# The last layer norm of a decoder step: sample tile in fifth place, small operations once per group, bias and gain spread over POOL and VectorE

## The chip, the cores and the metric

The kernel runs on one core of a Trainium2 chip. The metric is the device time of one execution in microseconds (us), as the median of several runs of the whole program. The five engines of the core run side by side and meet only at semaphores: TensorE (PE), VectorE (DVE), ScalarE (ACT), GpSimd (POOL) and SyncE (SP), which here issues the DMA transfers between HBM and the on-chip memory.

## The reference, cut to what matters

One layer of a decoder: a mixer, a layer norm, a mixture of experts and a second layer norm, for a prompt of 2048 rows and for 8 x 8 = 64 sample rows, each row 1024 wide. The change touches the last line only:

```python
u2 = x * (1.0 + sc2[:, None]) + sh2[:, None]
y_moe = _hier_moe(u2, w_group, b_group, w_route, b_route, w_gate, w_up, w_down)
x = _layer_norm(ALPHA * x + (1.0 + g2[:, None]) * y_moe, ln2_g, ln2_b)
# _layer_norm: (x - mean) * rsqrt(var + LN_EPS) * g + b, over each row
```

## The kernel before

The program is written engine by engine: every engine has its own instruction list (the functions under `@block.sync`, `@block.gpsimd`, `@block.scalar`, `@block.vector`, `@block.tensor`), and its order is the order of the code. Semaphores join them. `o.step` issues an instruction and makes its engine wait until it has finished; `o.did` only counts it, and `o.wait` waits later.

The stages follow one another: modulation vectors, projections and recurrence in eight chunks, output projection with the first layer norm, routing, 48 slots of 128 rows through the experts, and the last stage, which is the one changed. In the slots POOL scatters each result row into the residual sum `z_d` in HBM (prompt rows are added there) or into `ysamp_d` (the two expert results of each sample row). The last stage waits until all of it has landed.

The last stage works on NT = 17 tiles of up to 128 rows x 1024, each in its own buffer `zt[t]`. Tiles 0 to 15 are the prompt, tile 16 has the 64 sample rows. For one tile:

1. SP loads it (line 487; sample rows line 488, and their two expert results `y_pair` line 490). All loads are issued at the start, in the order of the tiles, the sample rows last; SP waits for the last scatter into `ysamp_d` (`yr0`, `yr1`) ahead of load 13.
2. DVE takes its statistics (`f_stats`): two `bn_stats` of 512 columns (line 1434), `bn_aggr` (1437) and adding epsilon to the variance (1438). For the sample tile three operations on 64 x 1024 stand ahead: the sum of the two expert results (1430), times the gate `g2_s` (1431), plus the residual rows (1432).
3. ACT takes the root (`root`, 918). DVE forms the reciprocal and minus mean times reciprocal (`f_scale`, 1444 and 1445).
4. ACT normalizes the tile (`norm_z`, 922), POOL multiplies it by the row `ln2_g` (`scale_o`, 662), DVE adds the row `ln2_b` (`f_out`, 1451), and SP stores it (494; the sample tile 496).

On DVE the steps of three tiles are interleaved by hand: statistics of tile t, scale of tile t-1, bias of tile t-2.

```python
            for t in range(2, NT):
                f_stats(t, P if t < NT - 1 else NS)
                f_scale(t - 1)
                f_out(t - 2)
            f_scale(NT - 1, NS)
            f_out(NT - 2)
            f_out(NT - 1, NS)
```

POOL and ACT go through the tiles in order; a semaphore that counts up (`frs_ready`, `fnorm`, `fg_ok`, `fo_ok`) tells each how far the one before it is. SP's stores wait in the same order.

Of the kernel before, what the change touches and what calls it, by code (L numbers as in the profile page):

```python
# [5 lines left out]
P = 128  # L6
D = 1024
KD = D // P
SEQ, DEC_B, DEC_T = 2048, 8, 8
NS = DEC_B * DEC_T  # L10
NTOK = SEQ + NS
# [25 lines left out]
LN_EPS = 1e-5  # L37
LRU_C = 8.0
# [46 lines left out]
def build(nc, A):  # L85
    with ExitStack() as ctx:
# [37 lines left out]
        def part_at(off, *shape):  # L124
# [138 lines left out]
            fg_ok fo_ok fo_stored""".split()}  # L263
# [37 lines left out]
        def _(sp):  # L301
# [200 lines left out]
        def _(pool):  # L502
# [156 lines left out]
            def scale_o(t, n=P):  # L659

                pool.wait_ge(S["fnorm"], t + 1)
# [3 lines left out]
            for t in range(NT):  # L665
                scale_o(t, P if t < NT - 1 else NS)
# [3 lines left out]
        def _(act):  # L670
# [245 lines left out]
            def root(t, n=P):  # L916
                act.wait_ge(S["fvar_ready"], t + 1)
                act.activation(sd_z[0:n, t:t + 1], mv_z[0:n, t, 1:2], ACT.Sqrt).then_inc(S["fsd_ready"], 1)

            def norm_z(t, n=P):  # L920
                act.wait_ge(S["frs_ready"], t + 1)
                act.activation(zt[t][0:n, :], zt[t][0:n, :], ACT.Identity, bias=rs_z[0:n, t, 1:2],  # L922
                               scale=rs_z[0:n, t, 0:1]).then_inc(S["fnorm"], 1)

            root(0)
            for t in range(1, NT):
                root(t, P if t < NT - 1 else NS)
                norm_z(t - 1)
            norm_z(NT - 1, NS)


        @block.vector
        def _(dve):
# [490 lines left out]
            def f_stats(t, n=P):  # L1424

                dve.wait_ge(z_in[t], 16)
# [6 lines left out]
                for h in range(2):  # L1433
                    o.did(dve.bn_stats(st6[t % 2][0:n, h, :], zt[t][0:n, 512 * h:512 * h + 512]))  # L1434
# [364 lines left out]
```

## Time and profile before

| | |
|---|---|
| median of 3 runs | 1424.78 us (1421.13 to 1426.93) |
| the profiled execution | 1424.33 us |
| its span in the profile | 1422.6 us |
| last stage in the profile, from the first statistics to the end of the last bias | 1346.50 to 1419.22 us |
| busy in the whole span | PE 1184.7, DVE 901.3, ACT 535.7, POOL 545.4 us |
| busy from 1342.0 us to the end (80.6 us) | PE 0.0, DVE 68.1, ACT 24.5, POOL 40.6 us |

Times in a view are us from the start of the span, durations are us, mean durations of a group are ns. A row of a timeline gives the start, the duration, the engine, the line of the kernel, the operation, what it writes and reads, and in brackets how long the engine had stood idle and what ended that. The last stage is about 5% of the span, and no matrix product runs in it.

### The profile page before, as it was taken

To read this page: it belongs to the slowest core of one execution; us is meant where nothing else is said; L and a number is where in the kernel's file an instruction comes from. 1 tells how busy PE (TensorE), PEld (TensorE's weight loads), DVE (VectorE), ACT (ScalarE), POOL (GpSimd) and SP (SyncE) were. 2 spreads that over 40 slices of the span, in tenths; PEclk is the share of its full clock that TensorE was granted. 3 is DMA by queue.
4 is the path that set the end of the run, shared out by engine and by line. 5 is a ranking of instruction groups with operands and counts; after the bars stand their busy time and mean duration, and the time that the engine had idled before them with its cause. 6 is when DMAs were issued, how large, how long until landed. Compare 5 with 4: busy or idle time off the path is not lost. (4 is left out here: it accounts for less than half of the span.)

```text
span 1422.6 us, 23126 instructions
## 1 busy us (share of the span) xinstructions
PE 1184.7 (83%) x6473; PEld 952.0 (67%) x6474; DVE 901.3 (63%) x1824; ACT 535.7 (38%) x915; POOL 545.4 (38%) x545
## 2 busy tenths in 40 slices
PE   6697899999999866799999418999999999999400
PEld 1122699999999765688887317778778787788300
DVE  1114659898899848555655595556676666643398
ACT  0200453535544360222222204445556545533232
POOL 1012022112222043556565243455565455444264
PEclk9897899999999888899999658999999999999755
DMA  8990011011111055244444408888899798654582
GB/s 260 363 349 4 1 38 59 16 43 59 59 59 43 16 183 180 94 147 162 144 162 134 154 15 290 217 216 207 231 268 269 203 269 207 147 111 97 133 310 111
DMA packets 114671, 214.47 MB, mean 151 GB/s; under 512 B 17669, under 2 KB 67337, under 8 KB 114597
## 3 DMA queue, kind: packets, MB, share of 16 engines
q1 hardware_dynamic: 93903, 163.20, 33.5%
q0 software_dynamic: 20736, 50.89, 16.2%
q8 instruction: 15, 0.25, 0.1%
q14 instruction: 17, 0.14, 0.0%
HBM read 153.36 MB, written 85.96 MB: 168 GB/s over the span
## 5 line engine op out<-in xcount | busy, mean ns | idle before, releaser
L1523 PE MATMUL bank<-parts 128*128 128x256 f32 (+2 forms) x1616 | 570.0, 353 | 37.4 <-POOL parts L567 17.5
L1525 PE MATMUL bank<-parts 128*128 128x256 f32 (+2 forms) x1616 | 553.0, 342 | 0.0
L1524 PE MATMUL bank<-parts 128*128 128x256 f32 (+2 forms) x1616 | 552.3, 342 | 0.0
L1523 PEld LDWEIGHTS bank<-parts 128*128 128x128 f32 x1616 | 309.0, 191 | 78.5 <-issue 20.8
L1525 PEld LDWEIGHTS bank<-parts 128*128 128x128 f32 x1616 | 308.4, 191 | 35.6
L1524 PEld LDWEIGHTS bank<-parts 128*128 128x128 f32 x1616 | 309.3, 191 | 31.9
L1470 PE MATMUL bank<-ident,arena 128*128 128x128 f32 (+4 forms) x788 | 118.3, 282 | 26.2 <-DVE arena L1166 8.5
L1470 PEld LDWEIGHTS bank<-ident,arena 128*128 128x128 f32 (+4 forms) x788 | 94.3, 147 | 54.9 <-issue 11.6
L545 POOL TENSOR_TENSOR arena<-arena 128x256 f32<-128x256 f32 (+1 forms) x36 | 26.1, 728 | 270.3 <-DVE h_last L1082 247.5
L1351 DVE TENSOR_TENSOR parts<-arena,parts x90 | 104.8, 1220 | 17.9 <-ACT parts L855 17.9
L880 ACT ACTIVATE arena<-bank,w_now 128x512 f32<-128x512 f32 x96 | 66.1, 689 | 127.3 <-PE bank L1525 73.0
L1497 PE MATMUL bank<-ada_arena,cT 128*9 128x512 f32 x192 | 87.0, 615 | 18.3 <-DMA ada_arena<-in_w_ada 18.3
L1385 DVE SCALAR_TENSOR_TENSOR arena<-bank,w_now,arena 128x512 f32<-128x512 f32 x96 | 69.2, 749 | 49.8 <-PE bank L1525 49.8
L855 ACT ACTIVATE parts<-arena x90 | 88.7, 1056 | 4.9 <-DMA arena<-in_w_down 4.9
L633 POOL DMA_INDIRECT z_d<-arena,dst_now x48 | 80.8, 1684 | 19.3 <-issue 19.3
L703 ACT ACTIVATE arena<-bank,proj_b 128x256 f32<-128x256 f32 x64 | 30.4, 475 | 142.4 <-PE bank L1525 142.4
L585 POOL TENSOR_TENSOR arena<-arena 128x1024 f32<-128x1024 f32 (+1 forms) x17 | 57.0, 3350 | 52.2 <-ACT arena L804 52.2
L1139 DVE TENSOR_TENSOR arena<-bank,arena 128x512 f32<-128x512 f32 (+1 forms) x34 | 21.8, 683 | 86.2 <-PE bank L1525 86.2
L1497 PEld LDWEIGHTS bank<-ada_arena,cT 128*9 128x9 f32 x192 | 17.6, 93 | 85.9 <-issue 85.9
L1358 DVE TENSOR_TENSOR parts<-bank,parts 128x512 fp32r<-128x512 f32 x96 | 61.8, 685 | 7.8 <-ACT parts L860 7.8
L860 ACT ACTIVATE parts<-bank 128x512 fp32r<-128x512 f32 x96 | 52.2, 596 | 35.9 <-PE bank L1470 33.5
L567 POOL TENSOR_TENSOR parts<-arena,parts 128x1024 fp32r<-128x1024 f32 (+1 forms) x17 | 44.9, 2643 | 49.8 <-ACT parts L791 49.8
(258 smaller groups left out, 1544.5 us busy)
## 6 DMA issues: line engine op xcount, KB each, us to landing
ada_arena<-in_w_ada SPq DMA_DIRECT2D x12, 2048.0 KB, 11.0
arena<-in_w_gate SPq DMA_DIRECT2D x16, 1024.0 KB, 5.8
arena<-in_w_up SPq DMA_DIRECT2D x16, 1024.0 KB, 9.4
arena<-in_w_down SPq DMA_DIRECT2D x16, 1024.0 KB, 13.1
arena<-in_x_prompt SPq DMA_DIRECT2D x8, 1024.0 KB, 6.6
yT_d<-arena SPq DMA_DIRECT2D x16, 512.0 KB, 4.4
arena<-yT_d SPq DMA_DIRECT2D x16, 512.0 KB, 4.7
arena<-in_x_prompt SPq DMA_DIRECT2D x16, 512.0 KB, 3.3
```

The source lines that it names most:

```text
L585: o.step(pool.tensor_tensor(x1[b][0:n, :], z[b][0:n, :], row_tiles[0:n, 1, :], ALU.mult))
L633: pool.indirect_dma_start(out=z_d, out_offset=bass.IndirectOffsetOnAxis(ap=dst_now[b][:, 0:1], axis=0), in_=y_sb[b], in_offset=None, compu ...
L855: act.activation(part(w_hi, e & 1, n), raw_part(e & 1, n), ACT.Copy).then_inc(S["w_hi"], 1)
L880: act.activation(y_raw[b][:, 512 * h:512 * h + 512], bank[5 + h][:, :], ACT.Copy, scale=w_now[b][:, 0:1]).then_inc(S["y_act"], 1)
L1351: dve.tensor_tensor(part(w_lo, e & 1, n), raw_part(e & 1, n), part(w_hi, e & 1, n).bitcast(F32), ALU.subtract).then_inc(S["w_lo"], 1)
L1358: dve.tensor_tensor(xT_lo[:, k, :], bank[h][:, :].rearrange("p (k n) -> p k n", n=P), xT_hi[:, k, :].bitcast(F32), ALU.subtract).then_inc( ...
L1385: dve.scalar_tensor_tensor(y_sb[b][:, cols], bank[5 + h][:, :], w_now[b][:, 0:1], g2_row[:, cols], ALU.mult, ALU.mult).then_inc(S["y_dve"], 1)
L1470: return pe.transpose(out, in_, ident[0:rows, 0:rows])
L1497: last = pe.matmul(bank[n][0:NM, :], cT[:, k, :], w_ada[n][:, k, :], start=k == 0, stop=k == KD - 1)
L1523: pe.matmul(out, x_hi, w_hi, start=start, stop=False)
L1524: pe.matmul(out, x_hi, w_lo, start=False, stop=False)
L1525: return pe.matmul(out, x_lo, w_hi, start=False, stop=stop)
```

## The change

All in the last stage. A position q from 0 to 16 takes the place of the tile number in the semaphores and in the small arrays; `FIN_TILES` says which tile stands there.

- **Order.** The sample tile is worked fifth (q = 4). Its loads are issued fifth too, and with them goes the wait for the scatters into `ysamp_d`.
- **Groups.** Adding epsilon, root, reciprocal and minus mean times reciprocal run once for a group of 4, 4, 4, 3 and 2 tiles instead of once per tile, on as many columns. `mv_z` is set to 1.0 beforehand, because the grouped operations read all 128 rows of the sample's column.
- **Lag.** DVE's bias of a tile stands five tiles behind its statistics.
- **Bias on POOL.** For q = 2, 5, 8, 11 POOL also adds the bias, right behind its multiply.
- **Last tile on DVE.** For q = 16 DVE multiplies by `ln2_g` and adds the bias; POOL leaves this tile out.

```diff
+FIN_TILES = (0, 1, 2, 3, 16, *range(4, 16))
+FIN_GROUPS = ((0, 4), (4, 8), (8, 12), (12, 15), (15, 17))
+FIN_LAG = 5
+FIN_DVE_GAIN = (16,)
+FIN_POOL_BIAS = (2, 5, 8, 11)
...
-            for t in range(NT - 1):
-                if t == 13:
+            for q, t in enumerate(FIN_TILES):
+                if t < NT - 1:
+                    sp.dma_start(zt[t], x1_t[t]).then_inc(z_in[q], 16)
+                else:
                     for b in range(2):
                         sp.wait_ge(S[f"yr{b}"], 16 * (SLOTS // 2))
-                sp.dma_start(zt[t], x1_t[t]).then_inc(z_in[t], 16)
-            sp.dma_start(zt[NT - 1][0:NS, :], z_d[SEQ:NTOK, :]).then_inc(z_in[NT - 1], 16)
-            for k in range(2):
-                sp.dma_start(y_pair[k][0:NS, :], ysamp_d[k * NS:(k + 1) * NS, :]).then_inc(pair_in, 16)
-            for t in range(NT):
-                sp.wait_ge(S["fo_ok"], t + 1)
+                    for k in range(2):
+                        sp.dma_start(y_pair[k][0:NS, :], ysamp_d[k * NS:(k + 1) * NS, :]).then_inc(pair_in, 16)
+                    sp.dma_start(zt[t][0:NS, :], z_d[SEQ:NTOK, :]).then_inc(z_in[q], 16)
+            for q, t in enumerate(FIN_TILES):
+                if q in FIN_POOL_BIAS:
+                    sp.wait_ge(S["fo_pool"], FIN_POOL_BIAS.index(q) + 1)
+                else:
+                    sp.wait_ge(S["fo_ok"], q + 1 - sum(n < q for n in FIN_POOL_BIAS))
...
+            def affine_o(q, t, n=P):
+
+                pool.wait_ge(S["fnorm"], q + 1)
                 pool.tensor_tensor(zt[t][0:n, :], zt[t][0:n, :], ln2_g[0:n, :], ALU.mult).then_inc(S["fg_ok"], 1)
+                if q in FIN_POOL_BIAS:
+                    pool.wait_ge(S["fg_ok"], q + 1)
+                    pool.tensor_tensor(zt[t][0:n, :], zt[t][0:n, :], ln2_b[0:n, :], ALU.add).then_inc(S["fo_pool"], 1)
...
+            def roots_z(i, lo, hi):
+                act.wait_ge(S["fvar_ready"], i + 1)
+                act.activation(sd_z[:, lo:hi], mv_z[:, lo:hi, 1], ACT.Sqrt).then_inc(S["fsd_ready"], 1)
+
+            def norms_z(i, lo, hi):
+                act.wait_ge(S["frs_ready"], i + 1)
+                for q in range(lo, hi):
...
+                o.did(dve.bn_aggr(mv_z[0:n, q, :], st6[q % 2][0:n, :, :].rearrange("p a b -> p (a b)")))
+
+            def f_vars(lo, hi):
+
+                o.wait()
+                dve.tensor_scalar(mv_z[:, lo:hi, 1], mv_z[:, lo:hi, 1], LN_EPS / (ALPHA * ALPHA), None,
                                   ALU.add).then_inc(S["fvar_ready"], 1)
 
+            def f_scales(i, lo, hi):
+
+                dve.wait_ge(S["fsd_ready"], i + 1)
+                o.step(dve.reciprocal(rs_z[:, lo:hi, 0], sd_z[:, lo:hi]))
+                dve.scalar_tensor_tensor(rs_z[:, lo:hi, 1], mv_z[:, lo:hi, 0], -1.0, rs_z[:, lo:hi, 0],
                                          ALU.mult, ALU.mult).then_inc(S["frs_ready"], 1)
 
+            def f_out(q, t, n=P):
+
+                if q in FIN_DVE_GAIN:
+                    dve.wait_ge(S["fnorm"], q + 1)
+                    dve.tensor_tensor(zt[t][0:n, :], zt[t][0:n, :], ln2_g[0:n, :], ALU.mult).then_inc(S["fg_dve"], 1)
+                    dve.wait_ge(S["fg_dve"], FIN_DVE_GAIN.index(q) + 1)
+                else:
+                    dve.wait_ge(S["fg_ok"], q + 1)
+                if q not in FIN_POOL_BIAS:
+                    dve.tensor_tensor(zt[t][0:n, :], zt[t][0:n, :], ln2_b[0:n, :], ALU.add).then_inc(S["fo_ok"], 1)
+
+            o.step(dve.memset(mv_z[:], 1.0))
             dve.wait_ge(S["fin_in"], 32)
-            f_stats(0)
-            f_stats(1)
-            f_scale(0)
-            for t in range(2, NT):
-                f_stats(t, P if t < NT - 1 else NS)
-                f_scale(t - 1)
-                f_out(t - 2)
-            f_scale(NT - 1, NS)
-            f_out(NT - 2)
-            f_out(NT - 1, NS)
+            out = 0
+            for i, (lo, hi) in enumerate(FIN_GROUPS):
+                for q in range(lo, hi):
+                    f_stats(q, FIN_TILES[q], P if FIN_TILES[q] < NT - 1 else NS)
+                    if q == hi - 1:
+                        f_vars(lo, hi)
+                    while out <= q - FIN_LAG:
+                        f_out(out, FIN_TILES[out], P if FIN_TILES[out] < NT - 1 else NS)
+                        out += 1
+                f_scales(i, lo, hi)
+            while out < NT:
+                f_out(out, FIN_TILES[out], P if FIN_TILES[out] < NT - 1 else NS)
+                out += 1
```

The order of the instructions shows at three places what moved. The names in square brackets are the semaphores an instruction waits for; `st`, `mv_z`, `sd_z` and `rs_z` hold the statistics, `arena` the tiles, `ada_arena` the two expert results of the sample rows.

On DVE, one round of the loop before, here for the tile in place 2:

```order
L1434 BN_STATS st_0<-arena 128x6 [waits z_in2]
L1434 BN_STATS st_0<-arena 128x6
L1436 MEMSET spare 1x1 [waits dve_order]
L1437 BN_AGGR mv_z<-st_0 128x2
L1438 TENSOR_SCALAR mv_z<-mv_z 128x1 [waits dve_order]
L1444 RECIPROCAL rs_z<-sd_z 128x1 [waits fsd_ready]
L1445 SCALAR_TENSOR_TENSOR rs_z<-mv_z,rs_z 128x1 [waits dve_order]
L1451 TENSOR_TENSOR arena<-arena 128x1024 [waits fg_ok]
```

On DVE in the change, from the end of the first group to the first bias:

```order
L1451 BN_AGGR mv_z<-st_1 128x2
L1456 TENSOR_SCALAR mv_z<-mv_z 128x4 [waits dve_order]
L1462 RECIPROCAL rs_z<-sd_z 128x4 [waits fsd_ready]
L1463 SCALAR_TENSOR_TENSOR rs_z<-mv_z,rs_z 128x4 [waits dve_order]
L1444 TENSOR_TENSOR ada_arena<-ada_arena 64x1024 [waits pair_in,fin_s_in,z_in4]
L1445 TENSOR_TENSOR ada_arena<-ada_arena,arena 64x1024 [waits dve_order]
L1446 TENSOR_TENSOR arena<-arena,ada_arena 64x1024 [waits dve_order]
L1448 BN_STATS st_0<-arena 64x6 [waits dve_order]
```

The scale of the first tile stands behind the statistics of four tiles instead of two, and the three sample operations follow it at once, with the biases behind them.

On DVE, the end of the program before:

```order
L1451 TENSOR_TENSOR arena<-arena 128x1024 [waits fg_ok]
L1430 TENSOR_TENSOR ada_arena<-ada_arena 64x1024 [waits pair_in,fin_s_in,z_in16]
L1431 TENSOR_TENSOR ada_arena<-ada_arena,arena 64x1024 [waits dve_order]
L1432 TENSOR_TENSOR arena<-arena,ada_arena 64x1024 [waits dve_order]
L1434 BN_STATS st_0<-arena 64x6 [waits dve_order]
```

And in the change:

```order
L1451 BN_AGGR mv_z<-st_0 128x2
L1456 TENSOR_SCALAR mv_z<-mv_z 128x2 [waits dve_order]
L1462 RECIPROCAL rs_z<-sd_z 128x2 [waits fsd_ready,fg_ok]
L1463 SCALAR_TENSOR_TENSOR rs_z<-mv_z,rs_z 128x2 [waits dve_order]
L1475 TENSOR_TENSOR arena<-arena 128x1024 [waits fg_ok] x4
L1470 TENSOR_TENSOR arena<-arena 128x1024 [waits fnorm]
L1475 TENSOR_TENSOR arena<-arena 128x1024 [waits fg_dve]
```

Four biases, a multiply and a fifth bias now end the program on DVE; the sample operations are gone from there.

On POOL, the last stage before, with the last scatters ahead of it:

```order
L633 DMA z_d<-arena,dst_now 2240x1024
L635 DMA ysamp_d<-arena,dst_now 128x1024
L662 TENSOR_TENSOR arena<-arena 128x1024 [waits fnorm,fin_in]
L662 TENSOR_TENSOR arena<-arena 128x1024 [waits fnorm] x15
L662 TENSOR_TENSOR arena<-arena 64x1024 [waits fnorm]
```

And in the change:

```order
L671 TENSOR_TENSOR arena<-arena 128x1024 [waits fnorm,fin_in]
L671 TENSOR_TENSOR arena<-arena 128x1024 [waits fnorm] x2
L674 TENSOR_TENSOR arena<-arena 128x1024 [waits fg_ok]
L671 TENSOR_TENSOR arena<-arena 128x1024 [waits fnorm]
L671 TENSOR_TENSOR arena<-arena 64x1024 [waits fnorm]
L671 TENSOR_TENSOR arena<-arena 128x1024 [waits fnorm]
L674 TENSOR_TENSOR arena<-arena 128x1024 [waits fg_ok]
L671 TENSOR_TENSOR arena<-arena 128x1024 [waits fnorm] x3
L674 TENSOR_TENSOR arena<-arena 128x1024 [waits fg_ok]
L671 TENSOR_TENSOR arena<-arena 128x1024 [waits fnorm] x3
```

POOL has 20 operations of this size where it had 17: 16 multiplies and four biases.

## Rows read from the trace of the kernel before

**Rows 1.** The page: the chain that ended last, by engine.

```profile
DVE 5%; DMA 1%; PE 0%; issue 0%; POOL 0%; ACT 0%; DVEq 0%; POOLq 0%; SPq 0%
```

**Rows 2.** Timeline, one round of the last stage on DVE, ACT and POOL.

```profile
1357.61 1.22 DVE L1451 TENSOR_TENSOR arena<-arena 128x1024 f32<-128x1024 f32 x1
1357.63 1.24 ACT L922 ACTIVATE arena<-arena,rs_z 128x1024 f32<-128x1024 f32 x1 [0.64 <-DVE rs_z L1445]
1358.76 1.28 DVE L1434 BATCH_NORM_STATS2 st<-arena 128x6 f32<-128x512 f32 x2
1358.95 2.34 POOL L662 TENSOR_TENSOR arena<-arena 128x1024 f32<-128x1024 f32 x1 [1.37 <-ACT arena L922]
...
1360.31 0.15 DVE L1438 TENSOR_SCALAR mv_z<-mv_z 128x1 f32<-128x1 f32 x1
...
1360.57 0.73 DVE L1445 SCALAR_TENSOR_TENSOR rs_z<-mv_z,rs_z 128x1 f32<-128x1 f32 x1
1361.32 1.22 DVE L1451 TENSOR_TENSOR arena<-arena 128x1024 f32<-128x1024 f32 x1
```

**Rows 3.** Groups by line and shape, line 1445: count | busy us, mean ns | idle before.

```profile
L1445 DVE SCALAR_TENSOR_TENSOR rs_z<-mv_z,rs_z 128x1 f32<-128x1 f32 x16 | 11.9, 742 | 0.6
```

**Rows 4.** Timeline, the end of the last stage.

```profile
1403.29 1.21 DVE L1430 TENSOR_TENSOR ada_arena<-ada_arena 64x1024 f32<-64x1024 f32 x1
1403.48 3.22 POOL L662 TENSOR_TENSOR arena<-arena 128x1024 f32<-128x1024 f32 x1 [1.37 <-ACT arena L922]
1404.53 3.24 DVE L1431 TENSOR_TENSOR ada_arena<-ada_arena,arena 64x1024 f32<-64x1024 f32 x1
...
1412.38 4.63 POOL L662 TENSOR_TENSOR arena<-arena 128x1024 f32<-128x1024 f32 x2 [5.68 <-ACT arena L922]
1414.74 4.48 DVE L1451 TENSOR_TENSOR arena<-arena 128x1024 f32<-128x1024 f32 x2 [2.34 <-POOL arena L662]
1419.25 0.52 SPq L496 DMA_DIRECT2D result<-arena  x1
```

**Rows 5.** Lines 562 and 1076, earlier stage: durations ns min/median/max, first and last start.

```profile
L562 POOL TENSOR_TENSOR parts<-arena,parts x3: 2377/3342/3354, 524.8 to 530.4; 128x1024 fp32r<-128x1024 f32 x3
L1076 DVE TENSOR_TENSOR parts<-arena,parts x5: 1212/3370/3431, 525.6 to 535.9; 128x1024 fp32r<-128x1024 f32 x5
```

**Rows 6.** Timeline, the start of the last stage.

```profile
1346.50 1.29 DVE L1434 BATCH_NORM_STATS2 st<-arena 128x6 f32<-128x512 f32 x2 [10.56 <-DMA arena<-z_d]
1347.83 0.20 DVE L1437 BATCH_NORM_AGGREGATE mv_z<-st 128x2 f32<-128x12 f32 x1
...
1348.07 0.15 DVE L1438 TENSOR_SCALAR mv_z<-mv_z 128x1 f32<-128x1 f32 x1
1348.14 1.28 DVE L1434 BATCH_NORM_STATS2 st<-arena 128x6 f32<-128x512 f32 x2
...
1351.54 2.33 POOL L662 TENSOR_TENSOR arena<-arena 128x1024 f32<-128x1024 f32 x1 [11.78 <-ACT arena L922]
```

**Rows 7.** Timeline, first layer norm: from epsilon to the scale, DVE waiting for ACT.

```profile
763.04 0.15 DVE L1154 TENSOR_SCALAR mv<-mv 128x1 f32<-128x1 f32 x1
...
763.66 0.16 DVE L1157 SCALAR_TENSOR_TENSOR rs<-mv,rs 128x1 f32<-128x1 f32 x1
```

**Rows 8.** Half-microsecond stretches: busy us (count) by engine, PEclk, DMA share, GB/s.

```profile
1351.00:1351.50 0.50, 0.00 (x0) 0.00 (x0) 0.46 (x3) 0.39 (x1) 0.00 (x0) 0.50 0.99 410
...
1366.50:1367.00 0.50, 0.00 (x0) 0.00 (x0) 0.50 (x2) 0.00 (x0) 0.50 (x1) 0.50 1.03 213
```

**Rows 9.** Timeline of the DMA issues on SP, then issues by line, us to landing.

```profile
1342.85 8.77 SPq L487 DMA_DIRECT2D arena<-z_d  x16
...
result<-arena SPq DMA_DIRECT2D x1, 256.0 KB, 2.9
```

**Rows 10.** Timeline, routing stage: a tensor_scalar on 16 columns beside POOL's run.

```profile
816.32 14.42 POOL L606 TENSOR_TENSOR parts<-arena,parts 128x1024 fp32r<-128x1024 f32 x6 [18.76 <-ACT parts L842]
...
826.19 2.26 DVE L1253 TENSOR_SCALAR arena<-arena 128x16 f32<-128x16 f32 x1
```

More of the change, by code:

```diff
@@ L657, in _ @@
                 scatter(s, s % 2, (s + 1) // 2)
-            def scale_o(t, n=P):
-                pool.wait_ge(S["fnorm"], t + 1)
+            def affine_o(q, t, n=P):
+                pool.wait_ge(S["fnorm"], q + 1)
                 pool.tensor_tensor(zt[t][0:n, :], zt[t][0:n, :], ln2_g[0:n, :], ALU.mult).then_inc(S["fg_ok"], 1)
+                if q in FIN_POOL_BIAS:
+                    pool.wait_ge(S["fg_ok"], q + 1)
+                    pool.tensor_tensor(zt[t][0:n, :], zt[t][0:n, :], ln2_b[0:n, :], ALU.add).then_inc(S["fo_pool"], 1)
             pool.wait_ge(S["fin_in"], 32)
-            for t in range(NT):
-                scale_o(t, P if t < NT - 1 else NS)
+            for q, t in enumerate(FIN_TILES):
+                if q not in FIN_DVE_GAIN:
+                    affine_o(q, t, P if t < NT - 1 else NS)
         @block.scalar
@@ L913, in _ @@
             y_evac(s, 1, SLOTS // 2 - 1)
[L916 to L929, printed above, removed]
+            def roots_z(i, lo, hi):
[4 more added lines that the diff above has]
+                for q in range(lo, hi):
+                    t = FIN_TILES[q]
+                    n = P if t < NT - 1 else NS
+                    act.activation(zt[t][0:n, :], zt[t][0:n, :], ACT.Identity, bias=rs_z[0:n, q, 1:2],
+                                   scale=rs_z[0:n, q, 0:1]).then_inc(S["fnorm"], 1)
+            for i, (lo, hi) in enumerate(FIN_GROUPS):
+                roots_z(i, lo, hi)
+                norms_z(i, lo, hi)
         @block.vector
@@ L1433, in f_stats @@
                 for h in range(2):
-                    o.did(dve.bn_stats(st6[t % 2][0:n, h, :], zt[t][0:n, 512 * h:512 * h + 512]))
+                    o.did(dve.bn_stats(st6[q % 2][0:n, h, :], zt[t][0:n, 512 * h:512 * h + 512]))
                 o.wait()
                 dve.memset(spare[0:1, 0:1], 0.0)
-                o.step(dve.bn_aggr(mv_z[0:n, t, :], st6[t % 2][0:n, :, :].rearrange("p a b -> p (a b)")))
-                dve.tensor_scalar(mv_z[0:n, t, 1:2], mv_z[0:n, t, 1:2], LN_EPS / (ALPHA * ALPHA), None,
+                o.did(dve.bn_aggr(mv_z[0:n, q, :], st6[q % 2][0:n, :, :].rearrange("p a b -> p (a b)")))
@@ L1439, in f_stats @@
+            def f_vars(lo, hi):
+                o.wait()
+                dve.tensor_scalar(mv_z[:, lo:hi, 1], mv_z[:, lo:hi, 1], LN_EPS / (ALPHA * ALPHA), None,
                                   ALU.add).then_inc(S["fvar_ready"], 1)
-            def f_scale(t, n=P):
-                dve.wait_ge(S["fsd_ready"], t + 1)
-                o.step(dve.reciprocal(rs_z[0:n, t, 0:1], sd_z[0:n, t:t + 1]))
-                dve.scalar_tensor_tensor(rs_z[0:n, t, 1:2], mv_z[0:n, t, 0:1], -1.0, rs_z[0:n, t, 0:1],
+            def f_scales(i, lo, hi):
+                dve.wait_ge(S["fsd_ready"], i + 1)
+                o.step(dve.reciprocal(rs_z[:, lo:hi, 0], sd_z[:, lo:hi]))
+                dve.scalar_tensor_tensor(rs_z[:, lo:hi, 1], mv_z[:, lo:hi, 0], -1.0, rs_z[:, lo:hi, 0],
@@ new lines, in _ @@
+            o.step(dve.memset(mv_z[:], 1.0))
+            dve.wait_ge(S["fin_in"], 32)
+            out = 0
+            for i, (lo, hi) in enumerate(FIN_GROUPS):
+                for q in range(lo, hi):
[6 more added lines that the diff above has]
+                f_scales(i, lo, hi)
```

9 lines of the change are left out of this document (3 added, 6 removed).

## The prediction

> **What bounds the kernel now.** I read the chain that ended last first. Only its end matters for a change in the last stage, and there it runs on DVE alone: DVE holds 5% of the whole span, about the length of this stage, and POOL and ACT hold 0% [rows 1]. So by the chain the stage is bound by VectorE. The timeline of one round says what VectorE does in that time [rows 2]. The bias of a tile (1.22 us) starts at 1357.61 and the next at 1361.32, so a round takes 3.71 us. In it the scalar_tensor_tensor on one column (line 1445) shows 0.73 us. It should be small: it starts at 1360.57 and ends at 1361.30, and POOL's multiply, begun at 1358.95 and 2.34 us long, ends at 1361.29. All sixteen of these have a mean of 0.74 us [rows 3]. The operation stands still until POOL is done.
>
> The end of the stage shows the same with large operands [rows 4]. POOL asks for its multiply at 1403.48, while DVE adds two tiles until 1404.50; POOL takes 3.22 us instead of 2.34. DVE starts its next product at 1404.53 and takes 3.24 us: to POOL's end at 1406.70 and 1.07 us more. So **a DVE operation with two on-chip inputs and POOL's elementwise operation exclude each other**; each waits for the other's end. Statistics have one input and don't wait: they take their 1.28 us while a multiply runs [rows 2]. An earlier stage shows both engines with operations queued back to back: POOL's take up to 3.35 us, DVE's 3.37 in the median [rows 5]. That is one POOL operation and one DVE operation, about 2.27 and 1.10 us, in strict turn; neither is shut out.
>
> The resource that bounds the stage is therefore not VectorE but this turn-taking, which I call the port. A round of 3.71 us is 2.34 (POOL) + 1.22 (DVE) and 0.15 of gaps; the statistics and small operations lie beside POOL's multiply.
>
> **The change part by part.**
>
> *Small operations per group.* Twelve of the 17 sets of epsilon, root, reciprocal and line 1445 go. On DVE three of them cost about 0.15 us each, and line 1445 its wait. Beside POOL's multiply all of that is hidden, so their removal is worth only the gaps: in strict turn a round costs 3.37 us [rows 5] instead of 3.71, that is 0.34 us in each round where both engines have work queued. Whether they have is the question of the next steps.
>
> *Head.* Before, POOL starts at 1351.54 [rows 6]. Now four statistics come first. The first aggregate starts 1.33 us behind the statistics, which took 1.29 us there with POOL idle, and an instruction without a wait follows a small one by 0.07 us (1348.07 to 1348.14) [rows 6], so a tile takes about 1.41 us and the fourth aggregate starts at 1352.06; with a wait behind each (0.24 us) it would be 1352.5. Epsilon follows at 1352.3. From there to line 1445, with ACT's root between, the first layer norm took 0.62 us [rows 7]: 1352.9, done at 1353.05. ACT normalizes in 1.24 us [rows 2], and POOL asks at 1354.4, **2.9 us later** than before. For four columns instead of one I take the same durations.
>
> *Sample tile fifth.* Its three operations (3 x 1.22 us) leave the end, where POOL stood idle for 5.68 us [rows 4], and come to 1353. When has it landed? The first tile is there at 1346.50 [rows 6]. At 410 GB/s a 0.524 MB tile takes 1.28 us, the fourth is there at 1350.3. The sample transfers ran at 213 GB/s, last of all in the program before [rows 8]; 0.786 MB then take 3.6 us: 1353.9. SP issues 16 loads in 8.77 us [rows 9], fast enough. For the wait on `yr0` and `yr1`, moved from load 13 to load 4, the bounds are nothing and 5 us (load 13 was reached at about 1350, and no wait shows there); I take nothing, since it waits only for small scatters that were issued with those already waited for.
>
> So DVE begins the sample at 1353.9 and ends its first sum at 1355.15. POOL asked at 1354.4, as it did at 1403.48 [rows 4], and has the port next. The product and the last sum alternate with two multiplies (2 x 3.35 us): the sample rows are ready at 1361.85 where they would be at 1357.6 if nothing stood between.
>
> *From there to the second group.* Two statistics to 1364.7; bias 0 waits for POOL's first bias (q = 2), which runs from 1364.2 to 1366.5, and ends at 1367.6; statistics to 1369; bias 1 waits for multiply 3 and ends at 1371.0; statistics to 1372.4; small operations 0.24 + 0.62 + 0.16, ACT 1.24, gaps: POOL asks for multiply 4 at 1374.7. Its multiply 3 ended at 1369.9. **POOL is dry for 4.8 us**, the price of working in groups, of which bias 1 fills 1.1.
>
> *From 1374.7 to the end.* POOL has 12 multiplies (q = 4 to 15) and 3 biases, 15 x 2.3 = 34.5 us. DVE has ten biases, the last tile's multiply and its bias, 12 x 1.15 = 13.8. All 27 use the port: 48.3 us, or 1423.0. Before the third group POOL runs dry again: bias 6 waits for multiply 6, multiply 7 is already queued and goes first (as the second multiply did at about 1414.7, ahead of the bias waiting for the first [rows 4]), and the group's small operations come behind that bias. That leaves the port empty for about 1.7 us: 1424.7. At the last two groups a bias or queued multiplies bridge it.
>
> *Bias on POOL, last tile on DVE.* Both are in this sum. Four biases cost 2.3 us of the port on POOL instead of 1.15 on DVE: +4.6. The last tile's multiply goes the other way: -1.15.
>
> *Store.* The last store is a full tile instead of 64 rows; 2.9 us to landing before [rows 9]; I count no difference, with 1 us either way.
>
> *Sum.* The last bias ended at 1419.22 (1414.74 + 4.48 [rows 4]). The same accounting gives 1419.7 for the kernel before, so I take 0.5 off: 1424.2, **5.0 us later**. 1424.33 + 5.0 = 1429.3 for an execution like the profiled one, which lies 0.45 us below the median of the runs; I forecast **1429.0 us**, +0.3%. A measurement of this kernel tells apart about 0.5%, 7 us, so this counts as no change.
>
> **A rule that could move it.** Epsilon on one column took 0.15 us beside POOL's multiply [rows 2]: it didn't wait. On 16 columns the same operation took 2.26 us beside a run of POOL's [rows 10]: it did. The groups have 2 to 4 columns and lie between. I take the one-column row, the nearest. The Trainium skill, VectorE: DVE Perf Modes, section What auto-detection actually checks, says that a one-input operation uses both read ports if the outermost dimension that isn't one is even or equal in source and destination. By it the grouped epsilon would wait. In my schedule it meets a busy POOL at three of five groups, and the bias behind it waits for that same operation anyway; by the rule the sum would be under 1 us more.
>
> **The rivals.**
>
> *The port never stands empty.* If the sample lands by 1353.2, DVE's product comes ahead of POOL's first multiply, the sample is ready about 3 us sooner, and the second group is in time. At the limit all operations stand in one unbroken row from 1353.1: 20 x 2.3 + 17 x 1.15 = 65.6 us, end 1418.7, which is 0.5 us less than before, or 1424. For it speaks that only 0.7 us decides; against it the 213 GB/s. Between it and the forecast lie 1424 to 1426.5.
>
> *POOL runs dry at every group* (the slower side). The small operations of a group stand on DVE behind its last statistics, and in groups 3 and 4 behind a bias which waits for POOL. From aggregate to POOL's next operation it is 0.24 + 0.62 + 0.16 + 1.24 and gaps, 2.4 us. If the last three groups each pay it in full, where I charge 1.7 in all, that is 7.2 - 1.7 = +5.5: 1434.5. It decides where the group's epsilon starts less than 2.4 us before POOL's queue ends; the wait of [rows 10] at each group would push it there, and so would a late sample. Against it speak the biases on POOL at q = 8 and 11, which lengthen its queue just there.
>
> *The engines don't exclude each other with these operands.* Then POOL needs 1354.4 + 20 x 2.34 = 1401.2 and DVE about as long, with dry spells the end is near 1407, and the time 1412. The views in [rows 2 to 5] speak against it throughout.
>
> **How the numbers follow.** The forecast, 1426.5 to 1432, has 0.52; the port always full 0.27; dry at every group 0.17; no exclusion 0.04. Faster by over 0.5% (under 1417.7) comes from the last alone: 0.04. Slower by over 0.5% (over 1431.9) is the third: 0.17. Within: 0.79. The range goes from 1421.5, the full port less 2.5 us for the scatter of the runs, to 1434.5: outside lie the last rival and half of the third, and a little of the second.
>
> **What would show it.** The sample's product taking 3.2 us or more beside POOL's first multiply; POOL's first multiply at 1354 to 1355; a gap of 4 to 5 us on POOL ahead of its fifth multiply, a smaller one ahead of the ninth; biases on DVE of 1.2 to 3.4 us, never two POOL operations long; the last bias at about 1424. Wrong would be: POOL without gaps after its start (first rival), gaps at all four boundaries (second), or a POOL multiply of 2.34 us with a DVE addition wholly inside it (third).

## The result, and the profile after

| | before | changed |
|---|---|---|
| median of 18 runs each | 1423.08 us (1416.88 to 1426.93) | 1427.15 us (1423.82 to 1431.61) |
| the profiled execution, its span | 1424.33, 1422.6 us | 1426.49, 1424.6 us |
| last stage, first statistics to end of the last bias | 1346.50 to 1419.22, 72.72 us | 1343.93 to 1421.51, 77.58 us |

The ratio is 1.0033, with a 95% interval from 1.0021 to 1.0045: slower, by less than the 0.5% that the prediction counted as no change. The stage is 4.86 us longer. In this execution it begins 2.57 us earlier than in the one of before, so positions are compared below as distances from the stage's start.

In the chain that ended last, by engine, POOL has come in [rows 1]:

```profile
DVE 4%; DMA 1%; POOL 1%; PE 0%; ACT 0%; SPq 0%; issue 0%; DVEq 0%; POOLq 0%
```

The timeline of POOL in the last stage of the changed kernel (start, duration, line, operation, and in brackets the idle time before and what ended it; L671 is the multiply, L674 the bias; three of the four biases are left out):

```profile
1352.23 9.54 POOL L671 TENSOR_TENSOR arena<-arena 128x1024 f32<-128x1024 f32 x3 [15.10 <-ACT arena L938]
...
1364.14 3.33 POOL L671 TENSOR_TENSOR arena<-arena 128x1024 f32<-128x1024 f32 x1
1372.26 5.70 POOL L671 TENSOR_TENSOR arena<-arena 64x1024 f32<-64x1024 f32 x2 [4.79 <-ACT arena L938]
...
1381.21 4.64 POOL L671 TENSOR_TENSOR arena<-arena 128x1024 f32<-128x1024 f32 x2
1388.56 3.39 POOL L671 TENSOR_TENSOR arena<-arena 128x1024 f32<-128x1024 f32 x1 [2.72 <-ACT arena L938]
...
1394.34 7.91 POOL L671 TENSOR_TENSOR arena<-arena 128x1024 f32<-128x1024 f32 x3
1402.33 2.35 POOL L674 TENSOR_TENSOR arena<-arena 128x1024 f32<-128x1024 f32 x1
1404.64 12.26 POOL L671 TENSOR_TENSOR arena<-arena 128x1024 f32<-128x1024 f32 x4
```

Two brackets stand behind the start: POOL is dry for 4.79 us ahead of the second group's first multiply (the fifth) and for 2.72 ahead of the third group's (the ninth). At the last two groups there is none. Before, POOL had idled 1.37 us in each round [rows 2] and 5.68 at the sample tile [rows 4].

The timeline of DVE for the same stretch (L1444 to L1446 are the sample's three operations, L1456 the grouped epsilon, L1470 the gain of the last tile, L1475 the bias):

```profile
1343.93 1.29 DVE L1448 BATCH_NORM_STATS2 st<-arena 128x6 f32<-128x512 f32 x2 [10.58 <-DMA arena<-z_d]
...
1349.99 0.17 DVE L1456 TENSOR_SCALAR mv_z<-mv_z 128x4 f32<-128x4 f32 x1
...
1351.78 1.22 DVE L1444 TENSOR_TENSOR ada_arena<-ada_arena 64x1024 f32<-64x1024 f32 x1 [0.97 <-DMA arena<-z_d]
1353.03 3.26 DVE L1445 TENSOR_TENSOR ada_arena<-ada_arena,arena 64x1024 f32<-64x1024 f32 x1
1356.32 3.25 DVE L1446 TENSOR_TENSOR arena<-arena,ada_arena 64x1024 f32<-64x1024 f32 x1
...
1375.70 3.34 DVE L1475 TENSOR_TENSOR arena<-arena 64x1024 f32<-64x1024 f32 x1 [0.82 <-POOL arena L671]
...
1381.92 1.65 DVE L1456 TENSOR_SCALAR mv_z<-mv_z 128x4 f32<-128x4 f32 x1
1383.58 3.35 DVE L1475 TENSOR_TENSOR arena<-arena 128x1024 f32<-128x1024 f32 x1
...
1393.56 0.84 DVE L1456 TENSOR_SCALAR mv_z<-mv_z 128x3 f32<-128x3 f32 x1
...
1407.24 0.75 DVE L1456 TENSOR_SCALAR mv_z<-mv_z 128x2 f32<-128x2 f32 x1
...
1410.20 8.92 DVE L1475 TENSOR_TENSOR arena<-arena 128x1024 f32<-128x1024 f32 x4
1419.05 1.21 DVE L1470 TENSOR_TENSOR arena<-arena 128x1024 f32<-128x1024 f32 x1
1420.29 1.22 DVE L1475 TENSOR_TENSOR arena<-arena 128x1024 f32<-128x1024 f32 x1
```

The sample's product and last sum take 3.26 and 3.25 us, since POOL's first multiplies run beside them; alone on the port such an operation took 1.22 (line 1444). The gain and bias of the last tile, with POOL done, take 1.21 and 1.22. In the groups by line and shape of the same stage (count | busy us, mean ns | idle before) the waiting shows as length:

```profile
L671 POOL TENSOR_TENSOR arena<-arena 128x1024 f32<-128x1024 f32 (+1 forms) x16 | 46.8, 2945 | 22.6 <-ACT arena L938 22.6
...
L1475 DVE TENSOR_TENSOR arena<-arena 128x1024 f32<-128x1024 f32 x12 | 26.1, 2192 | 2.3 <-POOL arena L671 2.3
...
L1463 DVE SCALAR_TENSOR_TENSOR rs_z<-mv_z,rs_z 128x3 f32<-128x3 f32 x1 | 2.1, 2095 | 0.0
...
L1463 DVE SCALAR_TENSOR_TENSOR rs_z<-mv_z,rs_z 128x2 f32<-128x2 f32 x1 | 1.7, 1748 | 0.0
```

POOL's multiply took 2.34 us in a round of before [rows 2] and 2.95 in the mean here; DVE's bias 1.22 there and 2.19 here. Most of that added busy time is waiting for the other engine.

### The profile page after: what moved, and what is told of

Its sections match the earlier page's. It is cut to its first block and busy times, and to the rows that moved or that the text cites. A ratio compares the mean times of both kernels' runs of the same rounds, so it can differ in the third digit from the quotient of the medians.

```text
span 1424.6 us, 23083 instructions
## 1 busy us (share of the span) xinstructions
PE 1183.7 (83%) x6473; PEld 950.4 (67%) x6474; DVE 905.4 (64%) x1786; ACT 532.3 (37%) x903; POOL 560.2 (39%) x548
```

## The experiments

Account to be tested: DVE's operations with two on-chip inputs and POOL's exclude each other (the port), and working in groups leaves POOL dry. Rivals: the bias on POOL is what costs; the late sample is what costs; VectorE's own work is the bound, so that taking its operations off the port is worth nothing. "Stage" is always from the first statistics to the end of the last bias in the profiled execution, with 72.72 us before and 77.58 after. Ratios are to the kernel before.

### No bias on POOL

```diff
-FIN_POOL_BIAS = (2, 5, 8, 11)
+FIN_POOL_BIAS = ()
```

> The change with no bias on POOL (DVE adds all biases). Stage length means from the first statistics to the end of the last bias: 72.7 us before, 77.6 us in the change. Theory (one POOL operation and one two-input DVE operation never overlap, so a bias on POOL costs the shared port 2.3 us instead of 1.15): four biases move back, worth 4.6 us of port, of which about half comes back as POOL running dry earlier at the third and fourth group: stage 75 to 76 us, 2 us under the change and still 3 us over before. Rival (no exclusion, VectorE is the bound): DVE gets four biases of 1.22 us more, stage 4.9 us longer than the change, 82 us.

Measured: stage 78.3 us (1345.12 to 1423.43), ratio 1.0038 [1.0023, 1.0054]. A miss: with four fewer long operations the stage grew by 0.7 instead of shrinking. Timeline of the middle of the stage, POOL and DVE:

```profile
1373.45 10.28 POOL L671 TENSOR_TENSOR arena<-arena 64x1024 f32<-64x1024 f32 x4 [8.03 <-ACT arena L938]
...
1376.87 7.93 DVE L1475 TENSOR_TENSOR arena<-arena 64x1024 f32<-64x1024 f32 x1 [0.80 <-POOL arena L671]
...
1391.75 3.39 POOL L671 TENSOR_TENSOR arena<-arena 128x1024 f32<-128x1024 f32 x1 [8.02 <-ACT arena L938]
```

POOL is now dry for 8.03 and 8.02 us, not 4.79 and 2.72. The second group's first multiply starts 28.33 us after the stage's start (1373.45 - 1345.12), and in the changed kernel also 28.33 (1372.26 - 1343.93). POOL only ended sooner and waited longer for the same group, so there its bias had filled time in which it would have been idle. The third group starts 46.63 us after the stage's start, where it was 44.63. Just ahead of it stands a wait that no account had: the 64-row bias at 1376.87 lasts 7.93 us. POOL's run of four ends at 1383.73 and the bias 1.07 later, so the three multiplies queued behind POOL's first all went ahead of it. With its turn behind one of them it would have ended some 4.7 us sooner (2 x 2.34, an estimate), so this run does not price the bias on POOL by itself.

The same kernel was run once more, to see whether the long wait belongs to the order of work:

> The same kernel as the run without biases on POOL, for one more profile. There one bias of DVE (the sample tile's, 64 x 1024) stood for 7.9 us: POOL ran three multiplies past it that had been ready, where everywhere else DVE came in after one. If that belongs to this order of work, the same bias stands for 7 to 8 us again and the stage is 78 us; if it was an accident of that execution, it takes at most 3.4 us and the stage is 73 to 76 us, as I had expected of that run.

Measured: 1423.7 us beside 1421.86 of the kernel before, stage 78.3 us. The same bias, in the timeline of that run:

```profile
1372.15 7.94 DVE L1475 TENSOR_TENSOR arena<-arena 64x1024 f32<-64x1024 f32 x1 [0.80 <-POOL arena L671]
```

It came back within 0.01 us, so it is no accident of one execution.

### The bias one tile later

```diff
-FIN_LAG = 5
+FIN_LAG = 6
```

> The change with the biases six tiles behind the statistics instead of five. Nothing is added or removed, only the two biases that stood ahead of the second group's small operations become one. Theory (the dry spell of POOL of 4.8 us ahead of its fifth multiply comes from biases that wait for POOL and hold up the group's statistics behind them): the second group's small operations come about 1.9 us earlier, and one at each later group less: stage 74 us, 3.7 us under the change. Rival (the stage is bound by the sum of port time alone, dry spells cost nothing): no difference, 77.6 us.

Measured: stage 75.03 us, where about 74 was expected; ratio 1.0015 [0.9999, 1.003]. The two dry spells, in POOL's timeline:

```profile
1372.83 4.66 POOL L671 TENSOR_TENSOR arena<-arena 64x1024 f32<-64x1024 f32 x2 [2.79 <-ACT arena L938]
...
1387.73 3.40 POOL L671 TENSOR_TENSOR arena<-arena 128x1024 f32<-128x1024 f32 x1 [1.38 <-ACT arena L938]
```

They fall from 4.79 to 2.79 and from 2.72 to 1.38, by 3.3 in all, and the stage by 2.55. Nothing but the order on DVE was changed, so the dry spells are on the path, and part of them came from biases that stand ahead of a group's statistics.

### Both

> The change with both edits: no bias on POOL, biases six tiles behind the statistics. Taking the bias off POOL alone made the stage 0.7 us longer (78.3 us against 77.6) where I had expected it 2 us shorter; six tiles of lag alone made it 2.6 us shorter (75.0). Theory now (what decides is whether POOL stands dry ahead of a group, and biases on DVE ahead of the group's small operations wait for POOL and make it so; without POOL's biases its queue is shorter and a third real bias stands there): with six tiles of lag that third bias falls behind the group's small operations, and the freed port time shows: 73 to 75 us, at or under the 75.0 of the lag alone. Rival (a bias costs the stage the same on POOL as on DVE, whatever the order): 75.0 + 0.7 = 75.7 us or more.

Measured: stage 72.59 us, just under what was expected; ratio 0.999 [0.9972, 1.0008]. With a lag of six the bias off POOL is worth 75.03 - 72.59 = 2.4 us. That is half of the 4.6 of the sum; POOL is again dry for longer ahead of the fifth multiply (5.49 us, beside 2.79).

### The sample tile last

```diff
-FIN_TILES = (0, 1, 2, 3, 16, *range(4, 16))
+FIN_TILES = tuple(range(17))
```

The wait for `yr0` and `yr1` stands ahead of load 13 again; position 16, which DVE multiplies, is then the sample tile.

> The change with the sample tile back in the last place (it is then the tile that DVE scales, and SP waits for the sample scatters ahead of tile 13 as before); groups, lag and the four biases on POOL as in the change. Theory: POOL's dry spell ahead of its fifth multiply (4.8 us in the change) goes, since nothing but biases stands between the first two groups, but the three sample operations come back to the end, where POOL is dry instead: stage 76.5 to 78 us, no different from the change (77.6). Rival (the sample tile in fifth place is what makes the change slower than before): stage 73 us or less, as before.

Measured: stage 77.77 us, ratio 1.0042 [1.0029, 1.0055]. POOL's timeline, two of its idle spells:

```profile
1367.28 5.69 POOL L672 TENSOR_TENSOR arena<-arena 128x1024 f32<-128x1024 f32 x2 [1.37 <-ACT arena L939]
...
1414.43 3.12 POOL L672 TENSOR_TENSOR arena<-arena 128x1024 f32<-128x1024 f32 x1 [4.89 <-ACT arena L939]
```

The spell ahead of the fifth multiply shrinks from 4.79 to 1.37 us, so the sample's three operations were what made it long; a spell of 4.89 comes back at the end. The place of the sample moves the idle time from one end of the stage to the other and is worth nothing in sum.

### One input from PSUM, one operation at a time

These runs ask what an operation costs when it no longer excludes POOL. First the kernel before with line 1445 as an operation with one tensor input:

```diff
-                dve.scalar_tensor_tensor(rs_z[0:n, t, 1:2], mv_z[0:n, t, 0:1], -1.0, rs_z[0:n, t, 0:1],
-                                         ALU.mult, ALU.mult).then_inc(S["frs_ready"], 1)
+                dve.tensor_scalar(rs_z[0:n, t, 1:2], mv_z[0:n, t, 0:1], rs_z[0:n, t, 0:1], -1.0,
+                                  ALU.mult, ALU.mult).then_inc(S["frs_ready"], 1)
```

> The kernel before, where line 1445 (minus mean times reciprocal, one column) is a tensor_scalar with one tensor input instead of a scalar_tensor_tensor with two. Theory (its 0.73 us is waiting for POOL's multiply, not work, and the port bounds the round): it takes 0.15 us beside a running multiply, the scale reaches ACT 0.57 us earlier, but the bias behind it now waits for the same multiply: a round goes from 3.71 to about 3.6 us at most, stage 71 to 72.5 us, 0.2 to 1.7 us less. Rival (VectorE is the bound and line 1445 is slow of itself): removing 0.57 us in 16 rounds takes 9 us off if the new form is quick, or nothing at all if it also shows 0.73 us.

Measured: stage 71.84 us, ratio 0.9997 [0.9983, 1.0011]. Timeline, the first bias, the third multiply, and two rounds later on:

```profile
1356.04 3.35 DVE L1451 TENSOR_TENSOR arena<-arena 128x1024 f32<-128x1024 f32 x1 [1.85 <-POOL arena L662]
...
1362.69 2.34 POOL L662 TENSOR_TENSOR arena<-arena 128x1024 f32<-128x1024 f32 x1 [4.38 <-ACT arena L922]
...
1368.03 0.21 DVE L1445 TENSOR_SCALAR rs_z<-mv_z,rs_z 128x1 f32<-128x1 f32 x1
...
1369.60 2.36 POOL L662 TENSOR_TENSOR arena<-arena 128x1024 f32<-128x1024 f32 x1 [1.10 <-ACT arena L922]
...
1372.00 1.23 DVE L1451 TENSOR_TENSOR arena<-arena 128x1024 f32<-128x1024 f32 x1 [0.28 <-POOL arena L662]
...
1376.53 2.36 POOL L662 TENSOR_TENSOR arena<-arena 128x1024 f32<-128x1024 f32 x1 [1.10 <-ACT arena L922]
```

The 0.73 us of line 1445 [rows 2] become 0.21, with no wait, and the round shrinks from 3.71 to 3.46 us. The port doesn't hold it there: POOL's wait of 1.10 us is ended by ACT, and the bias starts 0.04 us behind the multiply of its own tile (1369.60 + 2.36), for which it waited. What holds it is the order on DVE, in a chain over two rounds: the multiply of a tile, its bias, the next statistics and small operations behind that bias, ACT, and the multiply two tiles on, 6.93 us (1376.53 - 1369.60). The stage gains only 0.88 us, since the start got worse: the first bias now stands behind the second multiply, for 3.35 us, and the third multiply starts 14.12 us after the stage's start (1362.69 - 1348.57) instead of 12.45 [rows 2].

Then the kernel before with the bias alone changed. ACT copies the row `ln2_b` once into two PSUM banks, and DVE adds it in two halves of 512, so that one input comes from PSUM and one from the on-chip SBUF:

```diff
+            for h in range(2):
+                act.activation(bank[h][:, :], ln2_b[:, 512 * h:512 * h + 512], ACT.Copy).then_inc(S["fb_ok"], 1)
...
-                dve.tensor_tensor(zt[t][0:n, :], zt[t][0:n, :], ln2_b[0:n, :], ALU.add).then_inc(S["fo_ok"], 1)
+                for h in range(2):
+                    cols = slice(512 * h, 512 * h + 512)
+                    dve.tensor_tensor(zt[t][0:n, cols], bank[h][0:n, :], zt[t][0:n, cols], ALU.add).then_inc(S["fo_ok"], 1)
```

> The kernel before (no groups, sample tile last, all biases on DVE), with the bias row in PSUM as in the run with the bias in PSUM: the biases leave the shared port, line 1445 with its two one-column inputs in SBUF stays on it. Theory: the bias of 1.23 us now runs beside POOL's multiply, but line 1445 still waits for the multiply to end, and only then can ACT normalize the next tile (1.24 us) for POOL: a round is 2.34 + 1.24 + gaps = 3.65 us instead of 3.71, stage 71 to 72.7 us, 0 to 1.7 us less. Rival (the bias is what counts, each bias taken off the port saves its 1.22 us): stage 53 to 55 us.

Measured: stage 71.88 us, ratio 0.9989 [0.9976, 1.0002]. Timeline, one round:

```profile
1369.48 2.34 POOL L662 TENSOR_TENSOR arena<-arena 128x1024 f32<-128x1024 f32 x1 [1.36 <-ACT arena L927]
...
1371.17 0.67 DVE L1450 SCALAR_TENSOR_TENSOR rs_z<-mv_z,rs_z 128x1 f32<-128x1 f32 x1
1371.85 1.29 DVE L1458 TENSOR_TENSOR arena<-bank,arena 128x512 f32<-128x512 f32 x2
```

The round is still 3.71 us, though no bias stands in POOL's way. What keeps it is a loop of its own: the small operation (now line 1450) waits for POOL's end, ACT's normalization waits for it, and POOL's next multiply waits for ACT, 1.36 us after its last. The 0.84 us that the stage is shorter come at the end alone: the last two multiplies start 65.93 us after the stage's start (1411.82 - 1345.89), and before 65.88 (1412.38 - 1346.50), and the last bias but one no longer waits for the last multiply.

Both together in the kernel before:

> The kernel before with both: bias row in PSUM, and line 1445 as a tensor_scalar with one tensor input. Now nothing that DVE does in a round uses the port. Theory: a round on DVE is 1.41 us statistics, 0.24 wait, three small operations of 0.07 to 0.2 and 1.15 to 1.23 us of bias, about 3.2 us, and the stage is bound by VectorE at last: 65 to 68.5 us, 4 to 8 us under before. Each half alone (line 1445 alone took 0.9 us off, the bias alone is expected to take at most 1.7) gives less than half of that. Rival (the two add up): stage 70 to 71 us.

Measured: stage 68.72 us, ratio 0.9976 [0.9962, 0.999], just above what was expected. Each alone is worth 0.88 and 0.84 us, both 4.00. Timeline:

```profile
1351.87 1.29 DVE L1458 TENSOR_TENSOR arena<-bank,arena 128x512 f32<-128x512 f32 x2 [1.86 <-POOL arena L662]
...
1356.46 2.35 POOL L662 TENSOR_TENSOR arena<-arena 128x1024 f32<-128x1024 f32 x1 [2.31 <-ACT arena L927]
...
1365.80 1.29 DVE L1458 TENSOR_TENSOR arena<-bank,arena 128x512 f32<-128x512 f32 x2 [0.58 <-POOL arena L662]
1366.58 2.35 POOL L662 TENSOR_TENSOR arena<-arena 128x1024 f32<-128x1024 f32 x1 [0.81 <-ACT arena L927]
...
1370.39 2.35 POOL L662 TENSOR_TENSOR arena<-arena 128x1024 f32<-128x1024 f32 x1 [1.47 <-ACT arena L927]
```

Four rounds take 13.93 us (1370.39 - 1356.46), 3.48 each: **with line 1445 off the port, taking the bias off too doesn't shorten the round** (3.46 with the bias still on it). The same chain over two rounds still holds it; every second bias waits for the multiply of its own tile, like that at 1365.80. Of the 3.12 us that this stage is shorter than with line 1445 alone, 2.06 come at the start: the first bias takes 1.29 us instead of 3.35, and the third multiply starts 12.06 us after the stage's start (1356.46 - 1344.40) instead of 14.12. Another 0.91 come behind the start of the last two multiplies (5.95 us from there to the end, and 6.86 there), as in the run before.

The same edit of the bias in the changed kernel:

> The change with the bias row copied once to PSUM by ACT, so that DVE's bias reads one input from SBUF and one from PSUM, in two halves of 512 columns (about 0.68 us each by the additions of that form in the first layer norm, 1.36 us together instead of 1.22). Theory (two inputs in SBUF are what makes DVE and POOL wait for each other): the biases run beside POOL's operations at 0.68 us each half, POOL's multiplies are 2.34 us each wherever no sample or small operation stands in their way, stage 66 to 68 us, 10 us under the change and 6 us under before. Rival (VectorE is the bound): 13 biases of 0.14 us more, stage 79 us. Second rival (DVE and POOL exclude each other whatever DVE reads): the halves show waits of up to 2.3 us and the stage is 79 us or more.

Measured: stage 69.08 us, 8.5 less than the changed kernel, ratio 0.9939 [0.992, 0.9959]. Timeline:

```profile
1357.63 3.25 DVE L1450 TENSOR_TENSOR ada_arena<-ada_arena,arena 64x1024 f32<-64x1024 f32 x1
...
1366.32 2.34 POOL L671 TENSOR_TENSOR arena<-arena 128x1024 f32<-128x1024 f32 x1
1367.02 1.23 DVE L1482 TENSOR_TENSOR arena<-bank,arena 128x512 f32<-128x512 f32 x2
...
1374.55 4.67 POOL L671 TENSOR_TENSOR arena<-arena 64x1024 f32<-64x1024 f32 x2 [5.89 <-ACT arena L943]
```

The stage is 1.1 us longer than the upper end of what was expected; the dry spell ahead of the fifth multiply is still there, with 5.89 us. The bias lies inside POOL's multiply, and both have their undisturbed length; the sample's product, still with two SBUF inputs, waits as before. In one kernel the wait goes with the place of one input. Halves with both inputs in SBUF were not run; that the size isn't what counts is seen at line 1445, which waits with one column and two inputs and doesn't with one input. The Trainium skill, SBUF — State Buffer, section Who interferes with whom, says this as a rule: a VectorE instruction with two SBUF inputs contends with a GpSimd one that reads SBUF, one with a single SBUF input outside the two-port modes doesn't. These rows agree. So VectorE and GpSimd, which were said to meet only at semaphores, meet at this port too.

### A version built on it

From the changed kernel: groups as they are, lag six, sample last, all multiplies on POOL and all biases on DVE with one input from PSUM, epsilon as the bias of ACT's root, and the scale with one tensor input, once per tile. It changes much at once and isn't meant to tell the parts from each other.

```diff
+                act.activation(sd_z[:, lo:hi], mv_z[:, lo:hi, 1], ACT.Sqrt, bias=eps_z[:, 0:1]).then_inc(S["fsd_ready"], 1)
...
+                for q in range(lo, hi):
+                    dve.tensor_scalar(rs_z[:, q, 1:2], mv_z[:, q, 0:1], rs_z[:, q, 0:1], -1.0,
+                                      ALU.mult, ALU.mult).then_inc(S["frs_ready"], 1)
```

> Put together from the findings: groups as in the change, biases six tiles behind, sample tile last, all multiplies on POOL and all biases on DVE with the bias row in PSUM; epsilon goes into ACT's root as its bias, and line 1463 is one tensor_scalar on one column per tile. Nothing that DVE does uses the port except the three sample operations. Theory: DVE needs 17 x 1.41 us of statistics, 17 x 1.2 of biases, 3.7 for the sample and 3 to 4 for small operations, about 52 us in one row, with 1 to 3 us of waits; POOL's 17 multiplies are 2.34 us each: stage 53 to 57 us, 16 to 19 us under before, the whole run about 1.2% faster than before. Rival (POOL is the bound once the port is free, or the sample operations still block): stage 60 us or more.

Measured: stage 57.19 us, just above what was expected; ratio 0.9891 [0.9872, 0.9909]. What still waits are the sample's three operations, near the end. Timeline of DVE:

```profile
1384.63 2.81 DVE L1451 TENSOR_TENSOR ada_arena<-ada_arena 64x1024 f32<-64x1024 f32 x1
1387.48 3.25 DVE L1452 TENSOR_TENSOR ada_arena<-ada_arena,arena 64x1024 f32<-64x1024 f32 x1
1390.76 3.25 DVE L1453 TENSOR_TENSOR arena<-arena,ada_arena 64x1024 f32<-64x1024 f32 x1
```

So these, too, got one input from PSUM, copied there by ACT, which has time:

```diff
+                for out_t, first, op in ((y1, 4, ALU.add), (y1, 2, ALU.mult), (zt[t], 6, ALU.add)):
+                    for h in range(2):
+                        cols = slice(512 * h, 512 * h + 512)
+                        o.did(dve.tensor_tensor(out_t[0:n, cols], bank[first + h][0:n, :], y1[0:n, cols], op))
+                    o.wait()
```

> The version with one-input operations throughout, with the last three port users on DVE gone too: the gate of the sample rows, one of their expert results and their residual rows are copied to PSUM by ACT, and DVE's three sample operations read one input from there. In the run before them they took 2.8, 3.3 and 3.3 us beside POOL's multiplies. Theory (they waited for POOL): each takes 1.2 to 1.35 us, 5.5 us less in a row that DVE fills without a gap: stage 51 to 53 us against 57.2, the whole run 1.4 to 1.6% faster than before. Rival (POOL or ACT bounds it now, ACT having 3.6 us more of copies): 55 us or more.

Measured: 1404.19 us, ratio 0.9854 [0.9838, 0.9871], stage 53.1 us, again just above. Timeline of DVE at the sample:

```profile
1385.87 2.58 DVE L1472 TENSOR_TENSOR ada_arena<-bank,ada_arena 64x512 f32<-64x512 f32 x4
1388.49 1.28 DVE L1472 TENSOR_TENSOR arena<-bank,ada_arena 64x512 f32<-64x512 f32 x2
```

And the durations of all of POOL's multiplies (ns, min/median/max):

```profile
L673 POOL TENSOR_TENSOR arena<-arena x17: 2335/2348/2366, 1356.3 to 1396.5; 128x1024 f32<-128x1024 f32 x16, 64x1024 f32<-64x1024 f32 x1
```

Three operations that took 9.3 us take 3.9, and of the 17 multiplies the longest takes 2.37 us: none is stretched. This kernel is faster than both, before and changed.

## Why the prediction was right, and where it wasn't

**The forecast** was 1429.0 us and no change; measured are 1427.15, 0.3% over before.

**The bound.** For the changed kernel it holds that turn-taking and not VectorE's work is the bound: taking the bias off the port gave it 8.5 us with the same additions still on VectorE. For the kernel before, the reading of one round was wrong. I made the 3.71 us of POOL's multiply (2.34), the bias (1.22) and gaps. But with the bias off the port the round stays at 3.71, and with the bias left and line 1445 freed it falls to 3.46. The terms of the 3.71 were POOL's multiply, line 1445 ending with it, ACT's normalization (1.24) and gaps; that the normalization is as long as the bias beside it hid this. With both off the port and the order unchanged the round is still 3.48: turn-taking cost about 0.23 us of a round of before, and the chain over two rounds sets the rest. The sum for the change didn't rest on those terms, since the change removes most waits of line 1445; a forecast for the bias alone would have failed on them.

**Head.** The first multiply asks 8.30 us after the stage's start (1352.23 - 1343.93), the sum had 7.9.

**Sample tile.** First sum 7.85 us after the start, the sum had 7.4 (0.786 MB at its 213 GB/s are 3.7 us, not 3.6), and a DMA ends the wait of 0.97 ahead of it. SP issued the sample's loads at 1342.11, 0.10 us behind the fourth load, so the wait for `yr0` and `yr1`, taken as nothing, cost nothing. Product and last sum waited, at 3.26 and 3.25 us, as priced.

**The first dry spell** is 4.79 us where the sum had 4.8, and the sample at the end shortened it to 1.37. **The second** is 2.72, of which the bias at 1383.58 fills 1.1 (to 1386.93); the port stands empty for 1.6, and the sum had 1.7. At the last two groups none, as said. Lag six shows that these spells are on the path.

**The end.** The stage is 4.86 us longer, the sum had 5.0. The runs' medians differ by 4.07 us, the forecast by 1429.0 - 1424.78 = 4.2. This closeness is luck: the sum's 5.0 on that median is 1429.8, and the prediction gives no reason for 1429.0, nor does it show how it got 1419.7 for the kernel before. The rival with the port always full needed the product to start ahead of POOL's first multiply; it came 0.8 us behind it (1353.03 and 1352.23). The rival with POOL dry at every group needed dry spells at four boundaries. The one without exclusion needed a multiply of 2.34 us with an addition inside, which only the kernels with PSUM show.

**The step that failed: epsilon on a group.** I took the one-column row and no wait. Beside POOL it took 1.65 us on four columns, 0.84 on three and 0.75 on two; with POOL idle, at 1349.99, 0.17. It waited at three of the five groups, with two, three and four columns. The rule that stood beside the sum was right (the Trainium skill, VectorE: DVE Perf Modes, What auto-detection actually checks), and the trace agrees with it. That this costs under 1 us, since the bias behind waits for the same POOL operation anyway, is not shown: behind the 1.65 the bias asked at 1383.58, when POOL's next multiply had just begun (at about 1383.55, 1381.21 + 2.34), and waited for that one. No run changes epsilon alone. At the last two groups the scale behind it (line 1463) waited too, for 2.10 and 1.75 us, and there POOL had multiplies queued and no idle spell followed.

**Also failed: "in strict turn; neither is shut out".** In the changed kernel it held: durations of its biases (ns, min/median/max)

```profile
L1475 DVE TENSOR_TENSOR arena<-arena x13: 1170/2137/3370, 1362.4 to 1420.3; 128x1024 f32<-128x1024 f32 x12, 64x1024 f32<-64x1024 f32 x1
```

end at 3.37 us, one POOL operation and the bias itself. In two other kernels a bias waited for more than one: for three multiplies (7.93 and 7.94 us) and, with lag six, for two:

```profile
1374.24 4.33 DVE L1475 TENSOR_TENSOR arena<-arena 128x1024 f32<-128x1024 f32 x1
```

**The price of the bias on POOL**, +4.6 us in the sum, isn't confirmed as a term. At lag five taking it off made the stage longer by 0.7, the wait of 7.93 us included, at lag six shorter by 2.4. The first of the four biases cost nothing, since POOL would have been dry. The sum came out right in total, for this order of work; its terms can't be carried over to another order one by one.

So the change gained nothing because its parts cancel. The waits of line 1445 went away, but for two, and the idle end of the sample with them. In their place came 4.79 + 2.72 = 7.5 us of dry POOL ahead of two groups, a head that starts POOL 8.30 us after the stage's start instead of 5.04 [rows 6], and more work on the slower side of the port.

## What to carry to other kernels

Before moving work between VectorE and GpSimd, look for operations of the one that end just as those of the other do: there the two may share a resource, and an operation moved from VectorE (1.2 us) to GpSimd (2.3 us) may hold it longer (2.4 us for four of them here, at lag six). Giving the VectorE operation one input from PSUM took it off that resource here, and the kernel built on it throughout was 1.5% faster. Before a term is put into the sum of a round, ask which wait ends last: the bias was as long as the normalization beside it, and taking it away left the round as it was. Small operations done once per group make the engine behind them wait for the group's last member, so look at what stands between that member and the first result.

## What the runs showed that I had not expected

A VectorE operation that waits for the port isn't always next. In the kernel without bias on POOL, one that asked at 1376.87, while POOL's second multiply ran (it began at about 1383.73 - 3 x 2.34 = 1376.71), waited for that and two more; in the changed kernel none waited longer than 3.37 us, not even in the tail, where the last four biases (8.92 us) and POOL's last two multiplies took turns. What decides this is open. The 64 rows of the tile don't: with lag six a 128-row bias was passed over too, and in the changed kernel a 64-row one had its turn after one operation (3.34 us). No run was made to settle it.
